# Two of three out-projection chunks of a decoder layer as a Strassen-Winograd pair

## The reference

```python
h = rms_norm(x, g_attn[l])
proj = h @ w_in[l]
qa, ka, va, fa, qb, kb, vb, ga, gb = jnp.split(proj, offs, axis=-1)
...
merged = jax.nn.sigmoid(ga) * (o_a @ w_br_fox[l]) + jax.nn.sigmoid(gb) * (o_b @ w_br_dil[l])
x = x + merged @ w_out[l]
h = rms_norm(x, g_ffn[l])
u = h @ w_up[l]
...
x = x + (jax.nn.silu(gate) * val) @ w_down[l]
```

## Time and profile before

| | us |
|---|---|
| median of 3 runs | 1336.09 |
| lowest and highest run | 1335.77, 1336.88 |
| the profiled execution | 1335.9 |
| its span | 1333.9 |
| PE busy | 1329.0 |
| DVE busy | 1121.8 |
| ACT busy | 941.5 |
| POOL busy | 156.4 |

### The profile page before, as it was taken

The page is one execution under the profiler, slowest core; times in us unless marked ns, Lnnn a source line. Parts: engine busy times, 40 slices in busy tenths (PEclk is TensorE's granted clock), DMA queues, the critical chain, the costliest instruction groups (busy, mean ns, idle before and its releaser), DMA issues.

```text
span 1333.9 us, 16454 instructions
## 1 busy us (share of the span) xinstructions
PE 1329.0 (100%) x6055; PEld 1101.7 (83%) x6055; DVE 1121.8 (84%) x1334; ACT 941.5 (71%) x1181; POOL 156.4 (12%) x175
## 2 busy tenths in 40 slices
PE   9999999999999999999999999999999999999999
PEld 7888888888888888888888888888888888888887
DVE  6868787888888876657688898999999999999996
ACT  6666666666666654446777778888888888888872
POOL 0121212021011000001010101111111102020200
PEclk9999999999999999999999999999999999999999
DMA  9877685758888654667879688999989899999952
GB/s 357 285 176 255 143 268 115 246 145 239 229 219 227 206 177 171 213 228 224 273 171 335 159 301 171 314 219 283 245 254 268 229 288 213 302 209 311 202 192 106
DMA packets 118191, 305.73 MB, mean 229 GB/s; under 512 B 11864, under 2 KB 13152, under 8 KB 117600
## 3 DMA queue, kind: packets, MB, share of 16 engines
q1 hardware_dynamic: 92304, 234.57, 50.5%
q0 software_dynamic: 21728, 66.07, 27.8%
q10 hardware_dynamic: 4080, 4.05, 0.9%
HBM read 302.55 MB, written 2.11 MB: 228 GB/s over the span
## 4 chain that ended last, share of the span: by engine, by line
PE 98%; DMA 1%; DVE 0%; ACT 0%; issue 0%; SPq 0%; ACTq 0%
PE acc L746 13%; PE acc L750 13%; PE acc L748 13%; PE acc L786 9%; PE acc L790 9%; PE acc L788 9%; PE acc L973 4%; PE acc L977 4%; PE acc L975 4%; PE acc L948 3%; PE acc L950 3%; PE acc L952 3%; PE acc L1085 1%; PE acc L769 1%; PE acc L767 1%; PE acc L771 1%
## 5 line engine op out<-in xcount | busy, mean ns | idle before, releaser
L1776 DVE TENSOR_TENSOR w_lo<-raw,w_hi 128x1024 fp32r<-128x1024 f32 x233 | 282.6, 1220 | 89.2 <-ACT w_hi L1259 87.9
L1259 ACT ACTIVATE w_hi<-raw 128x1024 fp32r<-128x1024 f32 x233 | 243.7, 1054 | 110.2 <-PE acc L750 76.6
L746 PE MATMUL acc<-w_hi,actA 128*128 128x512 f32 x660 | 259.7, 394 | 0.1
L750 PE MATMUL acc<-w_hi,actA 128*128 128x512 f32 x660 | 257.3, 390 | 0.0
L748 PE MATMUL acc<-w_lo,actA 128*128 128x512 f32 x660 | 256.9, 389 | 0.0
L1259 ACT ACTIVATE w_hi<-raw_y 128x1024 fp32r<-128x1024 f32 x144 | 149.8, 1058 | 75.4 <-PE acc L750 22.6
L1776 DVE TENSOR_TENSOR w_lo<-raw_y,w_hi 128x1024 fp32r<-128x1024 f32 x144 | 173.2, 1219 | 23.4 <-ACT w_hi L1259 22.1
L1776 DVE TENSOR_TENSOR w_lo<-raw_x,w_hi 128x1024 fp32r<-128x1024 f32 x108 | 129.9, 1219 | 40.5 <-ACT w_hi L1259 40.1
L750 PEld LDWEIGHTS acc<-w_hi,actA 128*128 128x128 f32 x660 | 123.9, 188 | 26.1
L746 PEld LDWEIGHTS acc<-w_hi,actA 128*128 128x128 f32 x660 | 123.9, 188 | 25.5 <-issue 0.7
L748 PEld LDWEIGHTS acc<-w_lo,actA 128*128 128x128 f32 x660 | 124.0, 188 | 24.9
(11 more groups left out here) (300 smaller groups left out, 2606.9 us busy)
## 6 DMA issues: line engine op xcount, KB each, us to landing
raw<-w_in SPq DMA_DIRECT2D x101, 512.0 KB, 4.7
raw<-w_down SPq DMA_DIRECT2D x59, 512.0 KB, 5.6
raw_x<-w_up SPq DMA_DIRECT2D x44, 512.0 KB, 5.0
raw_y<-w_up POOLq DMA_DIRECT2D x34, 512.0 KB, 7.4
raw_x<-w_in SPq DMA_DIRECT2D x28, 512.0 KB, 4.0
raw<-w_out SPq DMA_DIRECT2D x28, 512.0 KB, 4.6
odd<-w_up SPq DMA_DIRECT2D x27, 512.0 KB, 5.1
work<-w_up SPq DMA_DIRECT2D x24, 512.0 KB, 5.5
```

The lines of the kernel that those rows point to most:

```text
L746: nc.tensor.matmul(o, lhsT=a_h, rhs=w_hi[:, s, k, :], start=first and k == 0, stop=False, skip_group_check=onto_seed)
L750: mm = nc.tensor.matmul(o, lhsT=a_l, rhs=w_hi[:, s, k, :], start=False, stop=last and k == KU - 1, skip_group_check=onto_seed)
L1259: nc.scalar.activation(w_hi[:, n % RING, :, :], src.rearrange("p (k n) -> p k n", k=KU), ACT.Copy).then_inc(hi_done, 1)
L1776: nc.vector.tensor_tensor(w_lo[:, n % RING, :, :], src.rearrange("p (k n) -> p k n", k=KU), w_hi[:, n % RING, :, :].bitcast(f32), ALU.subt ...
```

## The change

Chunks 0 and 1 of the out projection become an eighth pair, with the weights of `w_out` and the merged activation. Chunk 2 ("C") stays plain, on banks 6 and 7. The order of the 30 units is now a list: C0, P3 twice (once for each quad), C1, P1 twice, C2, P7 twice, P6 twice, G00, P5 twice, G01, G10, P2 twice, G02, P4 twice, G03, G11, G12, G13, C3 to C7; G10 is side 1, its first plain unit. Copies of merged chunks 0 and 1 go to `odd` for the sums (`make_merged`, four additions in a chain on DVE), and their high and low halves to `act_b` and `own_parts`. The x2 transposes stand behind G12 and C3. x is loaded in two halves. The FFN's first tiles for P2 and P4 are loaded behind the products whose buffers they take.

```diff
-FF_UNIT = OUT_UNIT + 3 * UPR
+    units = third(0) + product("P3") + third(1) + product("P1") + third(2) + product("P7") + product("P6")
+    units += plain(0, 0) + product("P5") + plain(0, 1) + plain(1, 0) + product("P2") + plain(0, 2)
+    return units + product("P4") + plain(0, 3) + plain(1, 1, 2, 3) + third(*range(3, UPR))
...
-OUT_BANKS = ((6, 7), (1, 3), (0, 2))
+OUT_BANKS = {"P3": 2, "P1": 0, "P7": 3, "P6": 0, "P5": 0, "P2": 1, "P4": 3}
...
+                elif name == "P2":
+                    sp.wait_ge(y_added[q], 2 * c + 2)
+                    load_b11(0, q)
+                elif name == "P4":
+                    sp.wait_ge(lo_done, n)
+                    load_b22(0, q)
...
+            def out_product(n, name, q):
+                if q == 0:
+                    if name == "P3":
+                        pe.wait_ge(dil_merged, 4)
+                        pe.wait_ge(h_part_lo, 5)
...
+            def out_plain(n, side, j):
...
+                for r, o in enumerate((bank[2], bank[0]) if side else (bank[1], bank[3])):
+                    if r and j == 0:
+                        pe.wait_ge(g_u0 if side else g_v7, PAIRS + 1)
...
+                    if unit == ("G", PAIRS, 1, 2):
+                        turn_x2(0)
...
+                    if u == 0:
+                        pe.wait_ge(g_c22, PAIRS)
+                        pe.wait_ge(mt_lo, 4)
...
+                    elif u == 3:
+                        turn_x2(1)
...
+                    elif c == 3 and u == 1:
+                        act.wait_ge(mt_lo, 2)
+                        merged_part_high("P3", 12)
+                        for half in range(2):
+                            nc.scalar.activation(own[:, 0, :, half * P:half * P + P],
+                                                 gate_quarter(0, 0, half).bitcast(f32), ACT.Copy, scale=-1.0)\
+                                .then_inc(h_part_hi, 1)
...
+                if name == "P1":
+                    act.wait_ge(dil_merged, 3)
+                    nc.scalar.activation(bank[1], bank[0], ACT.Copy, scale=-1.0).then_inc(g_p1, 1)
+                elif name == "P7":
+                    nc.scalar.activation(tmp[:, 1, :], bank[3], ACT.Copy).then_inc(g_v7, 1)
+                else:
+                    nc.scalar.activation(tmp[:, 0, :], bank[0], ACT.Copy, scale=-1.0).then_inc(g_v, 1)
+            for n, unit in enumerate(OUTS, OUT_UNIT):
+                if unit in (("H", PAIRS, "P1", QU - 1), ("H", PAIRS, "P7", QU - 1), ("H", PAIRS, "P6", QU - 1)):
+                    out_sum(n, unit[2])
...
+                elif unit == ("H", PAIRS, "P1", 0):
+                    act.dma_start(xr[:, :, 0:2 * NB], x_rows[:, :, 0:2 * NB]).then_inc(x_again, 16)
+                elif unit == ("H", PAIRS, "P5", 0):
+                    act.wait_ge(x_again, 16)
+                    act.dma_start(xr[:, :, 2 * NB:], x_rows[:, :, 2 * NB:]).then_inc(x_again, 16)
...
+                elif unit == ("C", 3):
+                    x2t_copy(1, bank[4:6])
+                    x2_squares(1)
...
+                    elif c == 3 and u == 0:
+                        make_merged()
+                    elif c == 3 and u == 2:
+                        merged_part_low("P3", 7)
...
+                if unit == ("H", PAIRS, "P5", QU - 1):
+                    dve.wait_ge(x_again, 16)
+                    dve.wait_ge(used, n + 1)
+                    add_bank(0, out_rows(0, 1)).then_inc(g_u0, 1)
...
+                elif unit == ("C", 4):
+                    make_sums()
+                elif unit == ("C", 6):
+                    part_low("P3")
+                    part_low("P1")
...
+            third_sum(PAIRS, 0)
+            third_sum(PAIRS, 1)
+            first_sum(PAIRS, 0)
+            first_sum(PAIRS, 1)
```

More of the change, by code:

```diff
@@ L110, with out_units, product, plain @@
 OUT_UNIT = BR_UNIT + 4 * UPR
-FF_UNIT = OUT_UNIT + 3 * UPR
+def out_units():
+    def product(name):
+        return [("H", PAIRS, name, q) for q in range(QU)]
+    def plain(side, *js):
+        return [("G", PAIRS, side, j) for j in js]
+    def third(*us):
+        return [("C", u) for u in us]
+    units = third(0) + product("P3") + third(1) + product("P1") + third(2) + product("P7") + product("P6")
+    units += plain(0, 0) + product("P5") + plain(0, 1) + plain(1, 0) + product("P2") + plain(0, 2)
+    return units + product("P4") + plain(0, 3) + plain(1, 1, 2, 3) + third(*range(3, UPR))
+OUTS = out_units()
+OUT_LOADS = [unit for unit in OUTS if unit[0] != "H"]
+OUT_LOAD_AT = {unit: k for k, unit in enumerate(OUT_LOADS)}
+OUT_AT = {unit: OUT_UNIT + n for n, unit in enumerate(OUTS)}
+FF_UNIT = OUT_UNIT + len(OUTS)
 GATE_PARTS = ("P3", "P5", "P6")
@@ L120, in raw_use, with pair_product @@
         k = GATE_LOAD_AT[GATES[n - GATE_UNIT]]
+    elif n < OUT_UNIT:
+        k = n - BR_UNIT + len(GATE_LOADS)
     else:
-        k = n - BR_UNIT + len(GATE_LOADS)
+        k = OUT_LOAD_AT[OUTS[n - OUT_UNIT]] + 4 * UPR + len(GATE_LOADS)
     return k % RAW_SLOTS, (GATE_UNIT + k) // RAW_SLOTS + 1
+def pair_product(n):
+    if GATE_UNIT <= n < BR_UNIT:
+        unit = GATES[n - GATE_UNIT]
+    elif OUT_UNIT <= n < FF_UNIT:
+        unit = OUTS[n - OUT_UNIT]
+    else:
+        return None
+    return unit if unit[0] == "H" else None
 def gate_banks(c):
@@ new lines, in out_plain @@
+            def out_plain(n, side, j):
+                pe.wait_ge(mt_lo, 6 if j < 2 else 8)
+                pe.wait_ge(lo_done, n)
+                s = n % RING
+                for r, o in enumerate((bank[2], bank[0]) if side else (bank[1], bank[3])):
+                    if r and j == 0:
+                        pe.wait_ge(g_u0 if side else g_v7, PAIRS + 1)
+                    for k in range(KU):
+                        kt = 2 * HK + KU * j + k
+                        a_h = actA[:, kt, r * P:(r + 1) * P]
+                        a_l = actA[:, kt, SEQ + r * P:SEQ + (r + 1) * P]
+                        nc.tensor.matmul(o, lhsT=a_h, rhs=w_hi[:, s, k, :], start=False, stop=False,
+                                         skip_group_check=True)
+                        nc.tensor.matmul(o, lhsT=a_h, rhs=w_lo[:, s, k, :], start=False, stop=False,
+                                         skip_group_check=True)
+                        mm = nc.tensor.matmul(o, lhsT=a_l, rhs=w_hi[:, s, k, :], start=False, stop=kt == KT - 1,
+                                              skip_group_check=True)
+                mm.then_inc(used, 1)
@@ new lines, in _ @@
+            for n, unit in enumerate(OUTS, OUT_UNIT):
+                if unit[0] == "H":
+                    out_product(n, unit[2], unit[3])
+                elif unit[0] == "G":
+                    out_plain(n, unit[2], unit[3])
+                    if unit == ("G", PAIRS, 1, 2):
+                        turn_x2(0)
+                else:
+                    u = unit[1]
+                    if u == 0:
+                        pe.wait_ge(g_c22, PAIRS)
+                        pe.wait_ge(mt_lo, 4)
+                    elif u == 4:
@@ L1782, in low @@
                 elif (n >= FF_UNIT and FFN[n - FF_UNIT][2] == "P7"
[L1783 removed]
+                      or pair and name == "P7"):
                     dve.wait_ge(lo_done, n)
@@ L2157, in add_x2, with out_rows @@
                 t.then_inc(x2_done, 1)
-            for c in range(3):
-                for u in range(UPR):
-                    if u == UPR - 1:
-                        if c == 0:
-                            dve.wait_ge(x_again, 16)
-                        add_x2(OUT_UNIT + UPR * c + u, c, [bank[b] for b in OUT_BANKS[c]])
-                    low(OUT_UNIT + UPR * c + u + RING)
-                    if u == 3 and c == 0:
-                        merged_low(3)
-                    elif u == 3 and c == 2:
-                        make_sums()
-                    elif u == 5 and c == 2:
-                        part_low("P3")
-                        part_low("P1")
-                    elif u == 6 and c == 2:
-                        part_low("P7")
-                        part_low("P6")
+            def out_rows(r, side):
+                return xr[:, r, side * NB:side * NB + NB]
@@ new lines, in _ @@
+            for n, unit in enumerate(OUTS, OUT_UNIT):
+                out_bank_sums(n, unit)
+                low(n + RING)
+                if unit == ("C", 0):
+                    merged_part_low("P7", 10)
+                elif unit == ("H", PAIRS, "P3", 1):
+                    merged_part_low("P6", 11)
+                elif unit == ("C", 1):
+                    merged_part_low("P5", 12)
+                elif unit == ("H", PAIRS, "P1", 0):
+                    merged_low(3)
+                elif unit == ("C", 4):
+                    make_sums()
+                elif unit == ("C", 6):
+                    part_low("P3")
+                    part_low("P1")
+                elif unit == ("C", UPR - 1):
+                    part_low("P7")
+                    part_low("P6")
```

202 lines of the change are left out of this document (149 added, 53 removed).

## The result

The changed kernel takes 1340.98 us in the median of six runs (1340.11 to 1341.90), the kernel before 1336.18. The ratio is 1.0036 with a 95% interval of 1.0023 to 1.0048: slower, by 4.8 us, and 0.2 us above the top of the range that was given. The profiled execution took 1341.34 us.

The account below looks back on a forecast made before the run. The prediction took TensorE (PE) to bound the kernel, busy 1329.0 of 1333.9 us. From 1335.9 us, -2.72 - 0.3 + 0.9 + 1.4 + 1.9 + 1.2 = +2.4 gave 1338.3 us, range 1335.2 to 1340.8.

Parts of the forecast that it names:

- the likeliest case: Whole kernel: time within 0.2% of the kernel before, 1333.4 to 1338.8 us; chance 0.53.
- (b): Before G00's second row, PE waits for ACT's copy of P7 out of bank 3: +1.4 us, ends 0 and 3.0.
- (d): Before the first FFN product, PE waits for P3's part from the x2 transposes: +1.2 us, ends 1.0 and 1.3.
- What leaves PE: Out projection: twelve matmuls fewer in chunks 0 and 1, -2.72 us, and no opening wait, -0.3 us.
- (a): P3 on bank 2 waits for DVE's branch products to free the bank: +0.9 us, with 0.7 to 1.1.
- C0 covers the bank: Rival at P3: the unit between hides the bank's evacuation, so no wait there; 1337.4 us, chance 0.04.
- the collision in full: Rival before G00's second row: x delays P5's second accumulation fully, landing 10.2 us or more after issue; 1340.2 us, chance 0.24.
- The rival with 3.0 us: The collision in full, with the wait before G00's second row at 3.0 us: 1340.2 us, chance 0.24.
- (c): Before G10's second row, PE waits for DVE to add P5's sum in bank 0 to x: +1.9 us, ends 1.0 and 2.2.
- the case without (b): Rival that x delays nothing: no wait before G00's second row, 1.5 us before G10's; 1336.5 us, chance 0.17.

Follow-up runs that it names:

- the last experiments: The changed kernel with x early, FFN parts earlier, C1 ahead of P3, early loads spread, P5's sum copied by ACT; lastly that copy placed sooner: 1333.35 us.
- x early: The changed kernel with ACT issuing the first half of x behind C0's unit, some 7.6 us earlier: 1337.92 us, ratio 1.0016 to the kernel before.

## Why the prediction was wrong

The direction of the sum was right and its size was not: +2.4 foretold, +4.8 measured, and the likeliest case, no measurable difference, did not come. In the profiled execution the first FFN product is 2.8 us later than foretold: 1.7 of that is (b), 1.0 lies ahead of the stage (0.67 and 0.32), 0.3 is (d), and the rest cancels.

- *What leaves PE* was right: -2.72 and -0.35, and the last experiments come to 1333.35, where 1336.2 less 3.1 is 1333.1.
- *(a)* was right in its chain and 0.18 too large: 0.72, in every run with P3 behind C0. That rules out the case in which C0 covers the bank. The Trainium skill ("Perfetto Trace Analysis", "Optimizing Tensor Performance") asks for rotation through banks; the measurement says that one unit of rotation, 2.72 us, was too little where the engine that empties the bank has a queue in front of it, and two units were enough (no pause in the three kernels with C1 ahead of P3).
- *(b)* is the term that failed: the landing of the second accumulation was sized too small. The chain up to it was right (issued 12.5 us after the last branch unit, foretold 12.6). The step took half of the 6.3 us by which 2 MB of x had delayed a load, 3.1, put it on the median landing of 6.2, and so had 9.3. It was 11.0, near the high end that the step named (10.9) and not its value. The base was too low: with x out of the way these transfers took 7.4 and 8.0 us (x early), not 6.2, and 1 MB of x added 3.0 to the second of them. So x's price was right and the landing it was added to was not. What makes 7.4 and 8.0 of 6.2 stays open; it hangs on the order of the stage, since with x early the three kernels with C1 behind P3 had 7.0 to 8.0 and the three with C1 ahead of it 6.0 to 6.8. The forecast's rival, the collision in full at 10.2 us and more, is the case that came, and it had got 0.24.
- *What the sum did not have* is the half clock behind the pause: 1.6 us in the profiled execution. The rival with 3.0 us came to 1340.2 and stopped there.
- *(c)* was right in size, 1.9 foretold and 1.87 to 1.95 where the clock stayed up, partly by luck: 1.5 was worked out for the case without (b), and it was 1.87 there (x early). And the sum had no clock in front of it. Behind the half clock only 0.36 was left of it. So the two errors cancel for the most part: the half clock and (c) are 1.96 together in the change and 1.95 with the clock up.
- *(d)* was 1.2 against 1.51, with 0.08 for the slow first distance. The releaser and the place were right.
- *Loads.* "the FFN's own loads for P2 and P4 are only issued earlier" was right, but the prediction passed over the change's four new loads in the branch projections. They cost PE 0.67 us in the profiled execution and nothing that the medians show.

The measured 1340.98 is outside the range by 0.2. It was not the clock that took it there: the terms of the stage as measured, the half clock among them, come to +4.2, and from 1335.9 to 1340.1, inside the range. The rest lies outside the stage: 0.67 and 0.32 ahead of it in the profiled execution. By the medians it is the 0.3 from 1335.9 to 1336.18 and the gap of 0.6 below the table of pauses, whose cause stays open. The first 60 us, which differ by 0.3 between the two profiles, were not tested. The burst was: without it the median was 0.14 lower and the gap still 0.5.

## What to carry to other kernels

A piece of arithmetic saved on the engine that bounds the kernel is worth what the new order of the others lets through: here 3.1 us were saved and 7.3 lost at four places, by the pauses and by the clock behind one of them, and four edits (x early, the FFN's parts earlier, C1 ahead of P3, one sum copied out by ACT), none of which touches a product, gave 7.2 of it back. Where a new transfer has a due time, list what else is issued on any queue until it has landed (11 us here), and move the one that has air (x was issued at 565.9 and first used by DVE at 588.1). And where a summed tile is due behind an in-order engine's wait, price the whole chain from the landing to the last engine, not the landing alone.
